# Four places instead of five for the rounded expert weights, with the order of the expert loop rewritten around them

## The reference, cut to what matters

```
def moe_ffn(h, w_router, b_router, w_g, w_u, w_d):
    ...                                    # each token is sent to 2 of 16 experts
    def expert_block(args):
        xb, e = args                       # the tokens of one expert, padded to a block
        return (jax.nn.silu(xb @ w_g[e]) * (xb @ w_u[e])) @ w_d[e]
    y_blk = lax.map(expert_block, (x_blk, block_e)).reshape(-1, d)
    ...                                    # weighted sum of each token's 2 results
```

## Time and profile before

| | us |
|---|---|
| median of 3 runs (2695.64 to 2700.96) | 2698.76 |
| the profiled execution | 2700.96 |
| its span, first to last instruction | 2699.1 |

### The profile page before, as it was taken

The page is one execution under the profiler, slowest core; times in us unless marked ns, Lnnn a source line. Parts: engine busy times, 40 slices in busy tenths (PEclk is TensorE's granted clock), DMA queues, the critical chain, the costliest instruction groups (busy, mean ns, idle before and its releaser), DMA issues.

```text
span 2699.1 us, 44061 instructions
## 1 busy us (share of the span) xinstructions
PE 2580.8 (96%) x16251; PEld 2173.3 (81%) x16251; DVE 1887.9 (70%) x2149; ACT 1511.8 (56%) x1543; POOL 181.7 (7%) x211
## 2 busy tenths in 40 slices
PE   5999998999999999999999999999999999999997
PEld 3756887878787878879897787899898977878995
DVE  3444767999999999975677575555456785756553
ACT  4433555888888888863556453443345564533432
POOL 0000010000000000000074000000000740000000
PEclk9999998999999999999999999999999999999999
DMA  7434636999999999964433025454544340254545
GB/s 284 161 151 157 225 141 256 400 413 407 408 411 405 411 403 413 403 275 169 156 144 138 34 102 203 172 188 160 193 171 146 140 152 34 102 203 172 188 156 195
DMA packets 79658, 610.09 MB, mean 226 GB/s; under 512 B 16004, under 2 KB 21700, under 8 KB 24968
## 3 DMA queue, kind: packets, MB, share of 16 engines
q1 hardware_dynamic: 79496, 607.87, 58.3%
HBM read 606.79 MB, written 1.05 MB: 225 GB/s over the span
## 4 chain that ended last, share of the span: by engine, by line
issue 48%; PE 33%; DVE 8%; POOL 6%; DMA 2%; ACT 2%; SPq 1%; DVEq 0%; POOLq 0%; ACTq 0%
PE psum_scalar L1801 4%; PE psum_scalar L1802 4%; DVE weight_slabs_rounded L1759 3%; PE psum_vector L550 3%; PE psum_vector L552 3%; PE psum_vector L551 3%; POOL arena L3543 3%; PE psum_scalar L550 2%; PE psum_scalar L551 2%; PE psum_scalar L552 2%; POOL arena L3546 2%; DVE arena_rounded L1759 2%; PE psum_vector L1773 2%; DMA weight_slabs<-in_mixer_slabs 1%; PE psum_scalar L1841 1%
## 5 line engine op out<-in xcount | busy, mean ns | idle before, releaser
L2202 DVE TENSOR_TENSOR weight_slabs_rounded<-weight_slabs,arena_rounded 128x2048 fp32r<-128x2048 f32 x208 | 477.9, 2307 | 342.5 <-ACT arena_rounded L2199 293.2
L2199 ACT ACTIVATE arena_rounded<-weight_slabs 128x2048 fp32r<-128x2048 f32 x208 | 396.4, 1913 | 361.6 <-PE psum_vector L552 223.5
L550 PE MATMUL psum_scalar<-arena_rounded,arena_rounded 128*128 128x256 f32 (+1 forms) x1456 | 472.6, 325 | 20.1 <-DVEq L1294 7.5
L550 PE MATMUL psum_vector<-arena_rounded,arena_rounded 128*128 128x512 f32 (+3 forms) x1264 | 456.2, 361 | 15.0 <-DVE weight_slabs_rounded L2202 14.9
L1759 DVE TENSOR_TENSOR weight_slabs_rounded<-weight_slabs,arena_rounded 128x2048 fp32r<-128x2048 f32 x192 | 430.9, 2285 | 9.0 <-DVE arena L1978 3.9
L1747 ACT ACTIVATE arena_rounded<-weight_slabs 128x2048 fp32r<-128x2048 f32 x192 | 362.2, 1910 | 38.5 <-PE psum_scalar L1802 19.8
L552 PE MATMUL psum_vector<-arena_rounded,arena_rounded 128*128 128x512 f32 (+1 forms) x896 | 348.0, 388 | 0.0
L551 PE MATMUL psum_vector<-weight_slabs_rounded,arena_rounded 128*128 128x512 f32 x880 | 343.8, 391 | 0.0
L550 PEld LDWEIGHTS psum_scalar<-arena_rounded,arena_rounded 128*128 128x128 f32 x1456 | 278.7, 191 | 52.4 <-issue 22.3
L1801 PE MATMUL psum_scalar<-arena_rounded,arena_rounded 128*128 128x512 f32 x768 | 307.9, 401 | 2.7
L550 PEld LDWEIGHTS psum_vector<-arena_rounded,arena_rounded 128*128 128x128 f32 (+2 forms) x1264 | 237.9, 188 | 54.6 <-DVE weight_slabs_rounded L2202 11.5
(11 more groups left out here) (497 smaller groups left out, 4138.8 us busy)
## 6 DMA issues: line engine op xcount, KB each, us to landing
weight_slabs<-in_layer_slabs SPq DMA_DIRECT2D x103, 2048.0 KB, 7.7
weight_slabs<-in_expert_slabs SPq DMA_DIRECT2D x192, 1024.0 KB, 8.2
arena<-in_expert_slabs SPq DMA_DIRECT2D x96, 1024.0 KB, 8.5
weight_slabs<-in_mixer_slabs SPq DMA_DIRECT2D x32, 2048.0 KB, 8.3
weight_slabs<-in_layer_slabs SPq DMA_DIRECT2D x6, 1024.0 KB, 5.5
arena<-in_mem SPq DMA_DIRECT2D x3, 1024.0 KB, 11.9
arena<-in_b_gate SPq DMA_DIRECT2D x6, 512.0 KB, 8.3
arena<-in_x SPq DMA_DIRECT2D x1, 1024.0 KB, 5.2
```

The costliest lines, as they stand in the source:

```text
L550: pe.matmul(out, left[0], right[0], start=start, stop=False)
L2199: e.activation(fr(high), low, ACT.Copy).then_inc(S("weights_high"), 1)
L2202: e.tensor_tensor(fr(low), low, fr(high).bitcast(F32), ALU.subtract).then_inc(S("weights_split"), 1)
```

## The change

- `HIGH_PLACES` has four places instead of five; the place at 64 KB is given up, and `actT`, `ye`, `gfin` and `xn2` move. `HIGH_PLACE` uses four places for h0 to h11 and three for h12 to h17. The copy of h1' now waits for h16 instead of h15, that of h2' for h17 instead of h16, that of h0' for h15 instead of h14. The first four copies of a block (`same` is empty) wait for no place.
- PE does h2 and h3 ahead of `combine` and the transposes, and `folded(2)` one half later.
- ACT and DVE have their small steps at other points among the halves: `choose_slots` comes ahead of low 8, `gathered` ahead of low 14.
- Before the loop DVE makes the low parts of h0, h1 and h2 ahead of `gathered`, where h1 and h2 stood behind it.
- The first two halves of the first layer's weights are split after the last block, on ACT behind `result(1)` (and one small activation), instead of inside it.

```
-        actT = fr(room(18, FE // P, P))
+        actT = fr(room(64, FE // P, P))
...
-            expert_halves(e, False, 0, (0,))
+            expert_halves(e, False, 0, (0, 1, 2))
             gathered(e, Banks(e, moe_vector_banks, ...), step)
-            expert_halves(e, False, 0, (1, 2))
...
-        HIGH_PLACES = (104, 112, 120, 32, 64)
-        HIGH_PLACE = [0, 1, 2, 3, 4] * 2 + [0, 1, 2, 3] * 2
-        LAST_PLACE = HIGH_PLACE[:12] + [2, 3, 4, 0, 3, 4]
+        HIGH_PLACES = (104, 112, 120, 32)
+        HIGH_PLACE = [0, 1, 2, 3] * 3 + [0, 1, 2] * 2
+        LAST_PLACE = HIGH_PLACE[:15] + [3, 0, 1]
...
-                    expert_high(e, i, h, (i + 1, same[-1]) if same else (i, before), places)
+                    expert_high(e, i, h, (i + 1, same[-1]) if same else None, places)
...
                 up_or_gate(0)
+                up_or_gate(1)
                 pe.wait_ge(S("ye_ready"), i + 1)
                 combine()
...
-                up_or_gate(1)
                 up_or_gate(2)
...
-                    if k == 2:
+                    if k == 4:
                         folded(2, 6)
...
-                    expert_high(e, i + 1, h, (i + 1, 14 + h))
+                    expert_high(e, i + 1, h, (i + 1, 15 + h))
...
-                high_parts(3, 4, 5)
+                high_parts(3, 4, 5, 6)
+                copied(0, 0)
+                high_parts(7)
...
-                if last:
-                    first_layer = Splitter(e, 0, high=True)
-                    for g, h in enumerate((12, 11)):
-                        half_read(e, i + 1, h)
-                        first_layer.upto(g)
-                else:
+                if not last:
...
-                low_parts(3, 4, 5, 6, 7, 8, 9)
+                low_parts(3, 4, 5, 6, 7)
...
-                low_parts(13, 14)
+                low_parts(13)
                 if not last:
                     gathered(e, V, step)
                 actT_low(1)
-                low_parts(15)
+                low_parts(14, 15)
...
         def act_between(e, last_):
+            weights = Splitter(e, 0, high=True)
+            for g, h in enumerate((14, 17)):
+                half_read(e, last_ + 1, h)
+                weights.upto(g)
```

More of the change, by code:

```diff
@@ L345, in build @@
         gate_up, gact = room(52, 2, 2, BANK), room(60, 2, 4, SLOTS)
-        actT = fr(room(18, FE // P, P))
-        ye = room(72, D)
-        gfin = room(76, D)
-        xn2 = room(80, NT, D)
+        actT = fr(room(64, FE // P, P))
+        ye = room(70, D)
+        gfin = room(74, D)
+        xn2 = room(78, NT, D)
         ss, rstd = tiny(16), tiny(16)
@@ L1754, in expert_halves @@
                     same = [q for q in range(h) if places[q] == places[h]]
-                    before = max(q for q in range(18) if HIGH_PLACE[q] == places[h])
-                    expert_high(e, i, h, (i + 1, same[-1]) if same else (i, before), places)
+                    expert_high(e, i, h, (i + 1, same[-1]) if same else None, places)
                 else:
@@ L1906, in one_block @@
                 e.sem_inc(S("selwT_ready"), 1)
-                copied(0, 0)
-                high_parts(6, 7)
                 copied(0, 1)
@@ L1911, in one_block @@
                 copied(1, 0)
-                high_parts(10)
                 silu(0)
-                high_parts(11)
+                high_parts(10, 11)
                 copied(1, 1)
-                rounded_act(0)
                 high_parts(12)
                 copied(2, 0)
+                silu(1)
+                rounded_act(0)
                 high_parts(13)
-                silu(1)
-                high_parts(14)
                 copied(2, 1)
-                high_parts(15)
                 rounded_act(1)
-                high_parts(16)
+                high_parts(14, 15, 16)
                 silu(2)
@@ L1991, in one_block @@
                     choose_slots(step, i + 1)
+                low_parts(8, 9)
                 multiply(0)
-                low_parts(10)
+                low_parts(10, 11, 12)
                 actT_low(0)
-                low_parts(11, 12)
                 multiply(1)
-                low_parts(13, 14)
+                low_parts(13)
                 if not last:
```

## The result

The changed kernel takes 2740.4 us (median of 4 runs, 2736.3 to 2741.7), the kernel before 2699.9 us (4 runs, 2695.6 to 2703.2): a ratio of 1.0151, 95% interval 1.0139 to 1.0165, or 40.5 us slower. The forecast was 2734.0, that is 35.2 us more than before.

The account below looks back on a forecast made before the run. DVE was taken to lead the loop, PE nearly as much. Loop 32.9, first block 1.2, last block -1.7 and behind it 2.8 sum to 35.2 us: 2734.0 from 2698.8, range 2726 to 2742 (chance 0.77).

Parts of the forecast that it names:

- The two meetings: Each loop block: DVE loses 0.35 us to ACT's late copy of h3' and 1.95 us waiting for PE's gather.
- loop block: Expert loop: a block takes 48.5 us instead of 46.25, taken as 2.35 more, for 14 blocks +32.9 us.
- ACT's wait at the copy of h15: Sign in the loop: ACT's 2.7 us wait for a place moves to the copy of h15.
- a PE wait at h1: Sign at a block's start: PE waits for DVE at h1, as at h2 and h3, the last near 0.9 us.
- First block and last block: The loop's two ends: first block +1.2 us; last block -0.1 us, and -1.6 for the slow stretch.
- The slow stretch: Last block, behind PE's 2.02 us wait at h16: 3.4 us at clock 0.53 goes away, -1.6 us (bounds 0 and -1.6).
- Behind the last block: After the second result: first layer's splits delay DVE's addition of the sums, +2.8 us; bound above, with a clock fall, 2.8 + 1.6.
- Rival (a): Gather wait in the loop is covered; only ACT's 0.35 to 0.5 us a block is left: 2707.5 us, chance 0.09.
- (b): DVE's queue never runs dry, so the new order gains: 2692.5 us, chance 0.05.
- slack of 0.14 at copy 17: End of a loop block: ACT's copy 17 is ready at 43.85, 0.14 us before DVE wants it at 43.99.
- (d): The transfers pace the loop, so a block stays at 46.25 us: 2700 us, chance 0.03.
- Rival (c): PE's new waits make the granted clock fall once in each loop block, 15 x 1.6 = 24 us more: 2758 us, chance 0.06.

Follow-up runs that it names:

- combine early: The changed kernel with PE doing `combine` and the transposes between h1 and h2 again: 2735.1 us, ratio 1.0135.
- four places alone: The kernel before with four places, later copy waits and the first layer's splits behind the last block, old loop orders kept: 2755.9 us, ratio 1.0199.
- five places, new orders: The changed kernel with places, memory and the first layer's splits as before, new orders of PE, ACT and DVE kept: 2727.1 us, ratio 1.0095.
- low 14 ahead: The changed kernel with h14's low part ahead of `gathered` on DVE again and its copy directly behind h13's: 2735.2 us, ratio 1.0135.
- two undone: The changed kernel with five places, `combine` between h1 and h2, and h14's low part and copy ahead of `gathered` again: 2708.6 us, ratio 1.0034.
- combine late alone: The kernel before with PE doing h2 and h3 ahead of `combine` and the transposes, ACT's list not matched: 2769.7 us, ratio 1.0262.
- the last experiment: The kernel before with h16's place in the last block's list changed from 3 to 1, first layer's second half copied when h16 is read: 2696.7 us, ratio 0.9990.
- splits alone: The kernel before with the first layer's two halves split behind the last block's second result instead of inside it: 2702.5 us, ratio 1.0013.

## Why the prediction was right, and where it was off

**DVE leads: the forecasts laid out from its queue held.** Add what DVE waits for other engines in a block to the 46.26 of before (less the 0.2 that it waited there):

| kernel | DVE waits for others | sum | measured block | expected block |
|---|---|---|---|---|
| changed | 2.14 + 0.62 | 48.8 | 48.88 | 48.5 |
| combine early | 1.38 + 0.62 | 48.1 | 48.44 | 48.3 |
| four places alone | 1.31 + 1.17 + 0.97 | 49.5 | 49.75 | 49.1 |
| five places, new orders | 2.15 | 48.2 | 48.39 | 48.3 |
| low 14 ahead | 1.86 + 0.55 | 48.5 | 48.64 | 48.5 |
| two undone | 0.72 | 46.8 | 46.97 | 46.95 |
| combine late alone | 4.41 | 50.5 | 50.77 | 50.7 |

The sum is 0.1 to 0.4 short (waits under 0.2 us are not among those read), and in the right order but for one pair that lies 0.05 apart. It is bookkeeping: a block is any engine's work plus its idle time, so it shows where DVE lost the time, not that DVE leads. For that speak the last column, laid out from DVE's queue before each run and within 0.4 us in six of seven kernels, and that DVE waited for other engines only 0.2 us a block before. After the change no engine leads alone: DVE waits for PE at the gather, and PE for DVE at h2, h3 and h16.

**The two meetings: right in place, mis-sized by 0.3.** Measured from h0, low h3' came at 646.73 - 642.09 = 4.64 (laid out: 4.81), PE's h3 at 6.98 (7.14), `combine` at 8.93 (8.96), the gather's end at 34.28 (34.43), the split at 34.51 (34.52), low h0' at 46.21 (46.21). But h0' itself came at 48.90 instead of 48.54: it waits 0.44 for `result(0)`, which no step had. I read that wait as a symptom. In the cycle that sets the pace, from one low h0' to the next, three steps were too short. The first matmul of a half that PE starts after a wait is followed at 0.34 us, not at 0.23 (649.07, 649.41, 649.64). This lies on the path at h3 (`combine` 1.95 behind h3's start, not 1.82). At h16, which also starts after a wait, the same step lies on it again: ACT's copy of h1' starts at 46.37, not 46.19, and hands 0.2 on to h3'. And DVE starts on the gathered tokens 0.23 behind PE's next product (676.37, 676.60), not 0.09. Against this, PE's way from `combine` to the gather's end was 0.12 shorter. Together 0.35 a block. All three repeat in the blocks of the loop (1.94 to 1.98, 46.3 to 46.4, and 0.23), but no run changed one of them by itself. The term "loop block" of 2.35 measured 2.63, and 14 x 0.28 = 3.9 of the 5.5 us by which the sum missed. Of the signs, ACT's wait at the copy of h15 (2.72) and the transfers' 387 GB/s (389 forecast) came; a PE wait at h1 did not, since h0 was late itself.

**First block and last block: right in the difference** (+1.3 and -2.0). For the first block that is partly luck: the layout had 45.7 and 46.8, the traces 46.07 and 47.36, both some 0.5 short. In the last block the wait at h16 fell from 2.02 to 0.36 and the clock stayed up. The prediction gave this to the new `LAST_PLACE`. The runs show two ways to it: the old list with the new orders also has 0.36 (five places, new orders), and the old orders with another list have no wait at h16 either (four places alone, and the last experiment). From its first product to the next `combine` the last block took 48.28 before, 46.31 after, 46.19 with the old list and the new orders, and 45.40 in the last experiment. The slow stretch was counted as if it came with the wait; "What the runs showed of the hardware" has waits of this length with and without it.

**Behind the last block: +2.8 right, and the bound above it came true.** PE's wait for the second slab grew from 1.90 to 3.59, and the clock fell to 0.50 for 3.4 us. I had this as a bound (2.8 + 1.6) and counted nothing; it cost 1.5. The run with these splits alone repeats both (2.3 for the clock), but with `combine` early the same wait of 3.58 left the clock at 1.00. So the 2.8 is a cost of the change, and the 1.5 one that an execution can have or not.

**Rival (a), the covered gather wait:** wrong; DVE waits there in all 14 blocks. **(b), DVE never dry:** wrong; the slack of 0.14 at copy 17 did hold, and yet DVE idled 2.8 us. **(d), the transfers:** wrong; the GB/s followed the block, with no ACT wait for a DMA in any loop read here.

**Rival (c), the clock:** wrong for the changed kernel. Over 680 us of its loop the granted clock is 1.00, with three PE waits of 0.4 to 0.8 us in each block. But in the kernel with four places alone, where one wait is 2.0 us, 9 of 15 blocks have a fall, the rival's own mechanism; each made its block 0.6 us longer on average, not the 1.6 that the rival counted. The Trainium skill ("TensorE: Matmul & The Clock Gate", section "A second HAM failure mode: psum-queue depth-cycling") has the clock swing where short idles between groups of matmuls are frequent. The section names no length and no number of idles, so whether three in 48.9 us are frequent is a reading. Read as the prediction read it, the changed loop would have swung; its trace does not agree. The kernel with four places alone does swing, and agrees with the cost that the rule names. What sets the two apart is not shown: the longer wait is one candidate, but six equal waits in the same loop had no fall behind them.

## What to carry to other kernels

When one engine leads by a few tenths, read its idle time and price every reordering by where that engine next meets an unfinished input; a wait that is filled with work comes back at the next meeting unless that input comes earlier too. Orders of several engines are worth something only as a set: a move that costs 0.4 us in one set cost 4.5 in another, and a smaller ring of buffers with old orders cost more (3.5 us a block) than with new ones (2.6). Look at the last pass of a loop by itself: one number in its list of places was worth 2.9 us in the trace, over half of it the slower clock behind a 2 us wait, which not every execution has.

## What the runs showed of the hardware

- A PE wait of one length was followed by a fall of the granted clock in one place and by none in another. The ten profiled executions, from block 0 of the loop to the first layer's start:

| PE's wait | before | clock fell behind it | stayed at 1.00 |
|---|---|---|---|
| 1.28 to 1.31 us | a half of the loop or the last block | 0 | 18 (16 with `combine` late alone) |
| 1.90 to 1.91 us | second slab of the first layer | 2 (`combine` late alone, two undone) | 3 |
| 2.02 to 2.03 us | h16 | 11 (before, splits alone, 9 with four places alone) | 7 (`combine` late alone, 6 with four places alone) |
| 3.58 to 3.59 us | second slab of the first layer | 4 (changed, four places alone, splits alone, low 14 ahead) | 1 (`combine` early) |

- So the length of the wait alone does not decide, and what else does was not tested. The shorter waits of the changed loop (0.4 to 0.8 us, three a block) had no fall in 680 us.
- Behind the last block a fall cost 1.5 us after the change, and 2.3 in the run with the splits alone, where the clock was also 0.86 in the 5.4 us behind the half-clock stretch.
- The first product after a wait is followed by the second 0.34 us after its start, against 0.23 in a running row.
- The loop's start moved by up to 4.3 us between profiled executions with nothing changed ahead of it (first `combine` at 452.13 before, 447.85 in the run with the splits alone). Spans therefore don't tell differences of 3 us; distances inside one trace do, as long as no fall of the clock lies in one of them and not in the other.
